# Two float32 transformer blocks in one program: the remaining projections in three rounded passes, split one job behind another, with a later bias table and two more expert buffers

## The chip, the cores and the metric

One core of a Trainium2 chip runs one program that computes both blocks. The metric is the device time of that program in microseconds (us). TensorE (PE) multiplies; VectorE (DVE), ScalarE (ACT) and GpSimd (POOL) do the elementwise work; SyncE (SP) issues nearly all DMAs.

## The reference, cut to what matters

All tensors are float32, with 256 tokens and a width of 1024. The first block has two layers of this form:

```python
for layer in range(2):
    u, q, k, v, g_pool, g_attn = split(rms(h, norm1) @ w_in)      # widths 1024, 3 x 1536, 1024, 1024
    pool_out = (centred_mean(u) - u) @ w_pool * pool_scale        # 4 groups of 256
    attn_out = dilated_attention(q, k, v, rel_bias)               # 12 heads of 128 in 3 groups, to 512
    h = h + (sigmoid(g_pool) * (pool_out @ w_a) + sigmoid(g_attn) * (attn_out @ w_b)) @ w_o
    a, gval = split(rms(h, norm2) @ w_up)                         # 2 x 2816
    h = h + (gelu(conv3(a)) * gval) @ w_down
```

The second block modulates its activations by `silu(c) @ w_ada`, mixes tokens in three ways, and ends in 32 experts of `(silu(x @ gate) * (x @ up)) @ down`, each 1024 by 512.

## The kernel before, in words

**Weights.** SP loads weights in blocks of 2 MB (`BLOCKS1`, L963) into `wring`, a ring of four slots (`SLOTS`). The load of block n waits until the last use of block n-4. `wb` blocks are half as large and `pool` blocks a quarter. Between the blocks of the first block lie twelve blocks `ada` of `w_ada`, which the second block needs; PE takes each in `modulate` (L1067) and adds it up in half of the PSUM tile `ps_s`.

**Jobs.** PE's work on a layer is a list of jobs (`layer_plan`). Each fills one of four PSUM banks, and begins when the bank of the job four places earlier is emptied. A layer has the jobs `x1` (transposes of the normed activations), 4 `u`, 6 `q`, 6 `k`, 6 `v`, 8 `gate` with the attention between them, 4 `pool`, 4 `wa`, 4 `wb`, 4 `wo`, `x2` (as `x1`), 22 `up` and 4 `down` that are accumulated in 11 rounds. Most jobs compute 256 output columns from half of a weight block, with K = 1024, which is eight tiles of 128 (`wb` has four).

**Split products.** The jobs u, q, k, v, up and down compute float32 products in three passes over rounded operands. ACT copies half a block, rounded, into `w_high` (two buffers, L1731, L1813); DVE subtracts it from the block to get `w_low` (L2106, L2202); activations are split into `x_high` and `x_low` in the same way. PE then makes three products for each tile (L1110): high by high, high by low, low by high. That is 48 matmuls of 256 columns for a job. ACT splits the weights of job n+2 as soon as job n is done. The jobs gate, pool, wa, wb and wo are ordinary float32 products (L1093, and L1199 for wo with 512 columns). The trace has two PE records for each float32 matmul, and one for each rounded matmul.

**Order at the norms.** After wo (or down), ACT squares the 256 by 1024 activations in two instructions and DVE scales them to `xs`. PE transposes them in the jobs x, ACT and DVE scale the transposed tiles out of PSUM into `xT`, ACT rounds all of it into `x_high` (L1738), and DVE subtracts it (L2111). Only then does the next product begin. PE takes three `ada` blocks ahead of these transposes, except in front of the first layer.

**Attention.** For each i of eight, PE computes `scores(i)`, the job `gate(i)`, the transposes of the probabilities of i-1 (`turn_probs`), and from the fourth on in every second the job `pv`. DVE does `logits(i)`: scale and bias (L2132), maximum, sign; after ACT's exponential it takes the reciprocal. ACT normalises (L1762), and takes the tanh of gate(i). DVE then copies the transposed probabilities of i-1 (`take_probT`, L2147). Each engine goes through its list strictly in order.

**Start.** Before layer 1 PE makes a table of attention biases; it goes out to DRAM, comes back with one row shifted per partition (`bias_table`), and PE mirrors it with twelve products by `flip`, which ACT copies out. DVE releases the first norm only then (L2042).

**Experts.** They are taken in eight turns of four, each turn with 12 blocks of 2 MB (L1017) in the four slots of `wring`. A load waits until `moe_used` says that its slot is free; the first four loads are released before the expert stage begins.

## Time and profile before

| | us |
|---|---|
| three runs | 2158.11, 2155.74, 2160.47 (median 2158.11) |
| the profiled execution's own time | 2155.31 |
| its span, first to last instruction | 2153.5 |
| PE busy | 1769.9 (82%) |
| DVE, ACT, POOL busy | 774.9 (36%), 545.7 (25%), 119.4 (6%) |

The mean granted TensorE clock is 0.925 of full speed. The program moves 417.76 MB by DMA, 194 GB/s on average. PE's busy share is an average over stages: in the first block PE is nearly always busy but at the norms and at the start, and in the expert stage it waits for weights. The part of the span outside of any stage below is the second block's mixing, which the change leaves in its order.

### The profile page before, as it was taken

The numbers are of one execution on the slowest core, as the hardware profiler recorded it, in microseconds if no ns is written. First come the engines' busy times: TensorE is split into PE (matmuls) and PEld (weight loads), VectorE is DVE, ScalarE is ACT, GpSimd is POOL, SyncE is SP. The second block draws the span as 40 slices with busy tenths as digits, with TensorE's granted clock in tenths as the row PEclk, the third lists the DMA queues.
The fourth block names the chain that finished last, engine by engine and source line by source line (L and its number), as shares of the span: only waits on it lengthen the run. The fifth ranks groups of instructions, "written<-read, shape, count | busy, mean of one in ns | idle before, by whom it ended". The sixth has DMA issues, their size and how long they took to land.

```text
span 2153.5 us, 30903 instructions
## 1 busy us (share of the span) xinstructions
PE 1769.9 (82%) x13683; PEld 1311.6 (61%) x13683; DVE 774.9 (36%) x1104; ACT 545.7 (25%) x708; POOL 119.4 (6%) x103
## 2 busy tenths in 40 slices
PE   2899997999799999799989998697984655566664
PEld 1899883997599987499767554486853111222221
DVE  0433212664434321366431744867533110111111
ACT  1443212543334320264321011333301100110110
POOL 0230000000041000000002410000000000000000
PEclk9899998999999999999999998798996888887898
DMA  6254156554755334575415110000033999999997
GB/s 238 102 177 163 50 176 258 200 179 155 274 192 176 121 108 181 197 260 211 178 57 142 64 39 10 1 3 2 32 137 128 409 409 409 410 409 391 405 409 298
DMA packets 154033, 417.76 MB, mean 194 GB/s; under 512 B 13799, under 2 KB 20746, under 8 KB 150847
## 3 DMA queue, kind: packets, MB, share of 16 engines
q1 hardware_dynamic: 151682, 412.65, 51.4%
q10 hardware_dynamic: 2236, 3.40, 0.5%
q8 instruction: 95, 1.56, 0.3%
q14 instruction: 20, 0.16, 0.0%
HBM read 414.14 MB, written 1.89 MB: 193 GB/s over the span
## 4 chain that ended last, share of the span: by engine, by line
PE 69%; DMA 21%; DVE 7%; ACT 2%; issue 2%; ACTq 0%; DVEq 0%; SPq 0%
PE bank L1110 24%; PE bank L1093 10%; DMA wring<-w_exp_down 7%; DMA wring<-w_exp_up 7%; PE bank L1229 6%; DMA wring<-w_exp_gate 4%; PE bank L1282 3%; PE bank L1199 3%; PE bank L1648 2%; PE bank L1307 2%; PE bank L1289 1%; PE ps_t L1282 1%; PE ps_t L1307 1%; PE ps_s L1307 1%; PE ps_s L1282 1%
## 5 line engine op out<-in xcount | busy, mean ns | idle before, releaser
L1110 PE MATMUL bank<-x_high,w_high 128*128 128x256 f32 x1216 | 346.3, 285 | 43.5 <-DVE x_low L2111 36.0
L1110 PE MATMUL bank<-x_low,w_high 128*128 128x256 f32 x1216 | 346.9, 285 | 0.0
L1110 PE MATMUL bank<-x_high,w_low 128*128 128x256 f32 x1216 | 340.2, 280 | 0.0
L2106 DVE TENSOR_TENSOR w_low<-wring,w_high 128x2048 fp32r<-128x2048 f32 x88 | 202.5, 2305 | 252.1 <-ACT w_high L1731 252.1
L1110 PEld LDWEIGHTS bank<-x_high,w_high 128*128 128x128 f32 x1216 | 231.2, 190 | 47.3 <-issue 47.3
L1110 PEld LDWEIGHTS bank<-x_high,w_low 128*128 128x128 f32 x1216 | 237.7, 195 | 0.0
L1731 ACT ACTIVATE w_high<-wring 128x2048 fp32r<-128x2048 f32 x88 | 168.6, 1920 | 271.9 <-PE bank L1110 263.2
L1110 PEld LDWEIGHTS bank<-x_low,w_high 128*128 128x128 f32 x1216 | 232.1, 191 | 0.0
L1648 PE MATMUL bank<-wring,R 128*32 128x512 f32 x1024 | 145.3, 707 | 89.5 <-DMA wring<-w_exp_up 76.0
L1093 PE MATMUL bank<-R,wring 128*128 128x256 f32 x704 | 155.2, 379 | 0.0
L1648 PEld LDWEIGHTS bank<-wring,R 128*32 128x32 f32 x1024 | 32.2, 122 | 196.3 <-DMA wring<-w_exp_up 116.1
L1093 PEld LDWEIGHTS bank<-R,wring 128*128 128x128 f32 x704 | 133.6, 190 | 18.1
L1664 PE MATMUL ps_s<-wring,R 128*32 128x512 f32 x256 | 48.2, 835 | 62.2 <-DMA wring<-w_exp_down 61.4
L2692 DVE TENSOR_TENSOR R<-bank,R 128x512 f32<-128x512 f32 x8 | 5.5, 692 | 227.1 <-PE bank L1648 227.1
L1282 PE MATMUL bank<-R,wring 128*128 128x512 f32 x176 | 79.4, 605 | 0.0
L1229 PE MATMUL bank<-w_high,a_high 128*128 128x512 f32 x176 | 70.1, 398 | 10.0 <-DVE R L2219 10.0
L2202 DVE TENSOR_TENSOR w_low<-wring,w_high 128x2048 fp32r<-128x2048 f32 x22 | 50.4, 2292 | 72.0 <-ACT w_high L1813 72.0
L2725 POOL TENSOR_TENSOR R<-R 128x542 f32<-128x542 f32 (+3 forms) x20 | 41.0, 2052 | 585.4 <-ACT R L1719 584.0
L1229 PE MATMUL bank<-w_low,a_high 128*128 128x512 f32 x176 | 70.0, 397 | 0.0
L1229 PE MATMUL bank<-w_high,a_low 128*128 128x512 f32 x176 | 69.8, 396 | 0.0
L1664 PEld LDWEIGHTS ps_s<-wring,R 128*32 128x32 f32 x256 | 5.7, 124 | 97.1 <-DMA wring<-w_exp_down 97.1
L1813 ACT ACTIVATE w_high<-wring 128x2048 fp32r<-128x2048 f32 x22 | 42.3, 1924 | 83.2 <-PE bank L1229 70.4
(549 smaller groups left out, 2683.0 us busy)
## 6 DMA issues: line engine op xcount, KB each, us to landing
wring<-w_in SPq DMA_DIRECT2D x37, 2048.0 KB, 8.1
wring<-w_exp_gate SPq DMA_DIRECT2D x32, 2048.0 KB, 17.4
wring<-w_exp_up SPq DMA_DIRECT2D x32, 2048.0 KB, 13.4
wring<-w_exp_down SPq DMA_DIRECT2D x32, 2048.0 KB, 17.5
wring<-w_up SPq DMA_DIRECT2D x22, 2048.0 KB, 9.0
wring<-w_ada SPq DMA_DIRECT2D x12, 2048.0 KB, 9.9
wring<-w_down SPq DMA_DIRECT2D x10, 2048.0 KB, 8.2
wring<-w_a SPq DMA_DIRECT2D x4, 2048.0 KB, 7.8
```

Of the source, the lines that this page charges most:

```text
L1093: mm = pe.matmul(b[:, i * S:(i + 1) * S], ww[:, wk0 + kk, c:c + P], rhs[0][:, rk0 + kk, :], start=kk == 0, stop=kk == rhs[1] - 1)
L1110: mm = pe.matmul(b[:, i * S:(i + 1) * S], left, right, start=k == 0 and m == 0, stop=k == KT - 1 and m == 2)
L1199: mm = pe.matmul(b[:, :], mT[:, k, t * P:(t + 1) * P], w(l, "wo", half, KT, 512)[:, k, :], start=k == 0, stop=k == KT - 1)
L1229: mm = pe.matmul(bank[JOB[("down", j)] % 4][:, :], left, ww[:, kk, half * 512:(half + 1) * 512], start=i == 0 and kk == 0 and m == 0, stop ...
L1282: mm = pe.matmul(b[:, i * width:(i + 1) * width], w2(n)[:, k, c:c + P], hT[:, k, 0:width], start=k == 0, stop=k == KT - 1)
L1307: mm = pe.matmul(b[q, 64 * o:64 * o + 64], lhs(q, c), rhs(q, c), start=start, stop=stop, skip_group_check=skip)
L1648: mm = pe.matmul(banks8[2 + which][q, :], xg[:, k, q], ww[:, u, k % 2, :], start=k == 0, stop=k == KT - 1)
L1664: mm = pe.matmul(banks8[5 + half][q, :], hidT[:, k, q], ww[:, u, half * 512:(half + 1) * 512], start=k == 0, stop=k == D_EXP // P - 1)
L1731: a.activation(w_high_r[:, n % 2, :, :], half_block(l, jobs[i], wring), ACT.Copy)\
L1813: a.activation(down_high(i), down_rows(l, i, wring), ACT.Copy).then_inc(w_high_ready, 1)
L2106: v.tensor_tensor(half_block(l, jobs[i], w_low), half_block(l, jobs[i], wring), w_high_r[:, n % 2, :, :].bitcast(F32), ALU.subtract).then_ ...
L2202: v.tensor_tensor(down_rows(l, i, w_low), down_rows(l, i, wring), down_high(i).bitcast(F32), ALU.subtract)\
```

## The change

1. The jobs gate, wa, wb and wo become split products too. One list `SPLITS` runs through u, q, k, v, gate, wa, wb, wo, up and down; ACT's `high(l, n)` and DVE's `low(l, n)` are called two jobs ahead everywhere. `split_rows` takes the operands, and alternates between the two halves of its bank in the innermost loop. pool stays float32.
2. The inputs of these products are split straight out of PSUM: ACT copies a bank, rounded, and DVE subtracts that from the same bank (`turned`, `pv_low`, and for the pooling output). The norms multiply by the gain before the transposes, in four products of 128x512 (`norm`, L2134 there), with the gain row loaded by DMA (`gain_row`). The squares are taken in pieces behind each job wo or down. A small Sqrt is put ahead of the place where the function table for it is needed.
3. The bias table is made behind the job u 3 of the first layer, with no mirroring; DVE reads it backwards. Its DMAs are issued by SP behind blocks k 0 and k 1.
4. `ada` blocks lie behind other blocks: two behind up 0 (or u 0) and one each behind the next two. PE takes two ahead of the transposes x2 (and x1 of the second layer) and two among the jobs.
5. `down` accumulates in `ps_s` and `ps_t`, and so does not wait for the banks of up.
6. The experts have six slots (`SLOTS_X`): two more in R, which grows by cutting the DMA scratch to 1024.

Cut to its core, the diff is:

```diff
+SLOTS, SLOTS_X = 4, 6
...
+DMA_SCRATCH = 1024
+R_SIZE = 36360
 
...
+    jobs = [("x1", j, "dve") for j in range(4)]
     jobs += [("u", j, "act") for j in range(4)]
...
 
 
 LAYER_BLOCKS = [("u", j, ("u", 2 * j + 1)) for j in range(2)]
@@ -94,14 +94,13 @@
 
     blocks = []
     for l in range(DEPTH):
+        behind = {}
+        if l:
+            behind.update({("u", 0): (4, 5), ("u", 1): (6,), ("q", 0): (7,)})
+        behind.update({("up", 0): (8 * l, 8 * l + 1), ("up", 1): (8 * l + 2,), ("up", 2): (8 * l + 3,)})
         for name, j, _ in LAYER_BLOCKS:
-            at = 2 * l + (name == "up") - 1
...
+SPLIT_MID = [(name, j) for name, n in (("gate", 8), ("wa", 4), ("wb", 4), ("wo", 4)) for j in range(n)]
 SPLIT_UP = [("up", j) for j in range(FT)]
 SPLIT_DOWN = [("down", i) for i in range(FT // 2)]
-SPLIT = {job: n for n, job in enumerate(SPLIT_IN + SPLIT_UP + SPLIT_DOWN)}
+SPLITS = SPLIT_IN + SPLIT_MID + SPLIT_UP + SPLIT_DOWN
+SPLIT = {job: n for n, job in enumerate(SPLITS)}
+NS = len(SPLITS)
...
+NORM_PARTS = (1, 4, 2, 4)
+SUMSQ_AT = [2 * sum(NORM_PARTS[:m]) for m in range(2 * DEPTH + 1)]
...
+        down_bank = [ps_s[:, 512:1024], ps_s[:, 0:512], ps_t[:, 0:512], ps_t[:, 512:1024]]
...
+            return (2 + m) % SLOTS_X
...
+            def gain_row(l, name):
+                sp.dma_start(grow, bass.AP(tensor=d[name].tensor, offset=l * D, ap=[[0, P], [1, D]])).then_inc(gain_in, 16)
...
+            gain_row(0, "norm1")
...
@@ -971,9 +1014,21 @@
                     for c, vec in enumerate(("c_2", "c_ctx_2")):
                         sp.dma_start(craw[:, c, :], bass.AP(tensor=d[vec].tensor, offset=0, ap=[[KT, P], [1, KT]]))\
                             .then_inc(craw_in, 16)
-                if (l, name, j) == (0, "up", 3):
+                if (l, name, j) == (0, "k", 0):
+                    sp.wait_ge(tab_ready, 1)
+                    sp.dma_start(tab_dram.rearrange("(g h) j -> h g j", h=4), tab[:, :, :]).then_inc(tab_out, 16)
+                if (l, name, j) == (0, "k", 1):
+                    sp.wait_ge(tab_out, 16)
+                    sp.dma_start(bias[:, :, :], bass.AP(tensor=tab_dram.tensor, offset=0,
+                                                        ap=[[1, P], [512, N_HEADS], [1, 384]])).then_inc(hankel_in, 16)
+                if (name, j) == ("wo", 1):
+                    wait_full(sp, l, ("pv", 3))
+                    gain_row(l, "norm2")
+                if (l, name, j) == (0, "up", 5):
+                    sp.wait_ge(xs_ready, 8)
+                    gain_row(1, "norm1")
                     set_out(0)
-                if (l, name, j) == (1, "q", 1):
+                if (l, name, j) == (1, "k", 1):
...
+                def split_rows(name, j, xh, xl, tokens_out=False, low_ready=None):
 
                     b = begin(name, j)
-                    ww = w(l, blk[0], blk[1], k, n)
-                    for i, c in enumerate((c0, c1)):
-                        for kk in range(rhs[1]):
...
-                    high, low = w_high_r[:, n % 2, :, :], half_block(l, (name, j), w_low)
-                    xh, xl = x_high_r, x_low_r
-                    for i in range(2):
-                        for k in range(KT):
-                            for m, (ww, xx) in enumerate(((high, xh), (high, xl), (low, xh))):
+                    wait_low(pe, l, (name, j))
+                    high, low = high_of(l, (name, j)), half_block(l, (name, j), w_low)
+                    last = k_tiles(name) - 1
+                    for k in range(last + 1):
+                        if low_ready and k % low_ready[1] == 0:
+                            pe.wait_ge(low_ready[0], l * HEADS_PER_GROUP + k // low_ready[1] + 1)
+                        for m, (ww, xx) in enumerate(((high, xh), (high, xl), (low, xh))):
+                            for i in range(2):
                                 part_of = slice(i * P, (i + 1) * P)
                                 left, right = (xx[:, k, part_of], ww[:, k, :]) if tokens_out else \
                                     (ww[:, k, part_of], xx[:, k, :])
-                                mm = pe.matmul(b[:, i * S:(i + 1) * S], left, right, start=k == 0 and m == 0,
-                                               stop=k == KT - 1 and m == 2)
+                                mm = pe.matmul(b[:, i * S:(i + 1) * S], left, right, start=k == 0 and m == 0 and i == 0,
+                                               stop=k == last and m == 2, skip_group_check=True)
+                    mm.then_inc(bank_full, 1)
...
-                pe.wait_ge(x_low_ready, l * 2 + 1)
...
+                for i in (8 * l, 8 * l + 1):
+                    modulate(l, i)
                 for j in range(4):
                     x_job("x2", j)
-                wait_emptied(pe, l, ("x2", 2))
-                wait_emptied(pe, l, ("x2", 3))
-                pe.wait_ge(x_low_ready, l * 2 + 2)
+                pe.wait_ge(x_low_ready, 4 * (2 * l + 2))
...
+            def high(l, n):
+
+                job = SPLITS[n]
+                wait_block(a, l, job[0], job[1] // 2)
+                if job[0] == "down":
+                    a.activation(down_high(l, job[1]), down_rows(l, job[1], wring), ACT.Copy).then_inc(w_high_ready, 1)
+                else:
+                    a.activation(high_of(l, job), half_block(l, job, wring), ACT.Copy).then_inc(w_high_ready, 1)
+
+            def root(l, n):
+                m = 2 * l + n
+                a.wait_ge(ms_ready, m + 1)
+                a.activation(stats[:, 12:14], stats[:, 10:12], ACT.Sqrt).then_inc(rms_ready, 1)
...
+            def turned(l, name, n):
+                for j in range(4):
+                    wait_full(a, l, (name, j))
+                    a.activation(half_tile(j, x_high), bank[JOB[(name, j)] % 4][:, :].rearrange("p (k s) -> p k s", s=P),
+                                 ACT.Copy).then_inc(x_high_ready, 1)
 
             for l in range(DEPTH):
...
+                a.activation(stats[:, 24:25], stats[:, 25:26], ACT.Sqrt)
+                for j in range(4):
+                    if j < 3:
+                        wait_full(a, l, ("wo", j))
+                        high(l, SPLIT[("wo", j)] + 2)
+                    wait_emptied(a, l, ("wo", j))
+                    for t in range(ST):
+                        c = slice(j * HALF, (j + 1) * HALF)
+                        a.activation(xn[:, t, c], h[:, t, c], ACT.Square, accum_out=stats[:, 4 * t + j:4 * t + j + 1]).then_inc(sumsq, 1)
+                root(l, 1)
+                turned(l, "x2", 1)
...
+            def low(l, n):
+
+                job = SPLITS[n]
+                wait_high(v, l, job)
+                if job[0] == "down":
+                    v.tensor_tensor(down_rows(l, job[1], w_low), down_rows(l, job[1], wring), down_high(l, job[1]).bitcast(F32),
+                                    ALU.subtract).then_inc(w_low_ready, 1)
+                else:
+                    v.tensor_tensor(half_block(l, job, w_low), half_block(l, job, wring), high_of(l, job).bitcast(F32),
+                                    ALU.subtract).then_inc(w_low_ready, 1)
...
+            def norm(l, n):
+
+                m = 2 * l + n
+                parts = NORM_PARTS[m]
+                v.wait_ge(sumsq, SUMSQ_AT[m + 1])
+                sums = stats[:, 0:2 * parts].rearrange("p (t c) -> p t c", t=ST)
+                if parts > 1:
+                    chain(v.tensor_reduce(stats[:, 8:10], sums, AX_X, ALU.add))
+                v.tensor_scalar(stats[:, 10:12], stats[:, 8:10] if parts > 1 else stats[:, 0:2], 1.0 / D, EPS, ALU.mult, ALU.add)\
+                    .then_inc(ms_ready, 1)
+                v.wait_ge(rms_ready, m + 1)
+                chain(v.reciprocal(stats[:, 14:16], stats[:, 12:14]))
+                v.wait_ge(gain_in, 16 * (m + 1))
+                for j in range(4):
+                    t, c = j // 2, slice((j % 2) * 512, (j % 2 + 1) * 512)
+                    v.scalar_tensor_tensor(xn[:, t, c], h[:, t, c], stats[:, 14 + t:15 + t], grow[:, c], ALU.mult, ALU.mult)\
+                        .then_inc(xs_ready, 1)
+
+            def turned(l, name, n):
+                for j in range(4):
+                    v.wait_ge(x_high_ready, 4 * (2 * l + n) + j + 1)
+                    v.tensor_tensor(half_tile(j, x_low), bank[JOB[(name, j)] % 4][:, :].rearrange("p (k s) -> p k s", s=P),
+                                    half_tile(j, x_high).bitcast(F32), ALU.subtract).then_inc(x_low_ready, 1)
+                v.wait_ge(x_low_ready, 4 * (2 * l + n) + 4)
+                for j in range(4):
+                    v.nop().then_inc(dve_emptied, 1)
 
             for l in range(DEPTH):
...
+                def pv_low(hh):
+                    v.wait_ge(at_high_ready, 4 * l + hh + 1)
+                    v.tensor_tensor(at_low[:, hh, :], bank[JOB[("pv", hh)] % 4][:, 0:S], at_high[:, hh, :].bitcast(F32),
+                                    ALU.subtract).then_inc(at_low_ready, 1)
+                    v.wait_ge(at_low_ready, 4 * l + hh + 1)
+                    v.nop().then_inc(dve_emptied, 1)
...
                     logits(i)
                     if i:
                         take_probT(i - 1)
+                    low(l, SPLIT[("gate", i)] + 2)
+                    if i % 2 == 0 and i >= 4:
+                        pv_low((i - 4) // 2)
...
+                def m_low(j):
+                    v.wait_ge(m_high_ready, 4 * l + j + 1)
+                    v.tensor_tensor(x_low[:, 2 * j:2 * j + 2, :], mT[:, 2 * j:2 * j + 2, :], x_high[:, 2 * j:2 * j + 2, :].bitcast(F32),
+                                    ALU.subtract).then_inc(m_low_ready, 1)
...
-                    wait_emptied(v, l, ("wa", j))
-                    v.tensor_tensor(m, m, tmp, ALU.add).then_inc(dve_emptied, 1)
                     wait_emptied(v, l, ("wb", j))
+                    v.tensor_tensor(m, m, tmp, ALU.add).then_inc(m_ready, 1)
+                    v.wait_ge(m_ready, 4 * l + j + 1)
+                    low(l, SPLIT[("wb", j)] + 2)
+                    if j:
+                        m_low(j - 1)
+                m_low(3)
                 for j in range(4):
...
+            v.memset(st[:, 61:62], 0.0).then_inc(moe_used, 2)
...
+    nc = bacc.Bacc("TRN2", target_bir_lowering=False, num_devices=1, dynamic_dma_scratch_size=DMA_SCRATCH)
```

DVE in the attention. Here is one i of the eight before: logits (four rows) and `take_probT`.

```order
L2132 SCALAR_TENSOR_TENSOR R<-ps_s,R 128x768
L2137 TENSOR_REDUCE stats<-R 128x1
L2138 TENSOR_SCALAR stats<-stats 128x1
L2140 RECIPROCAL stats<-stats 128x1
L2147 COPY R<-ps_t 128x6x128
```

And here is one i in the changed kernel, with the first row of the next.

```order
L2169 SCALAR_TENSOR_TENSOR R<-ps_s,R 128x768
L2174 TENSOR_REDUCE stats<-R 128x1
L2175 TENSOR_SCALAR stats<-stats 128x1
L2177 RECIPROCAL stats<-stats 128x1
L2184 COPY R<-ps_t 128x6x128
L2116 TENSOR_TENSOR w_low<-wring,w_high 128x8x256
L2169 SCALAR_TENSOR_TENSOR R<-ps_s,R 128x768
```

The subtraction for gate(i+2) now stands between the logits of i and those of i+1.

DVE at the second norm of a layer before, from the last updates of h by wo to the first jobs up.

```order
L2174 SCALAR_TENSOR_TENSOR h<-bank,h 128x512 x4
L2082 TENSOR_SCALAR stats<-stats 128x2
L2084 RECIPROCAL stats<-stats 128x2
L2086 TENSOR_SCALAR xs<-h,stats 128x1024 x2
L2106 TENSOR_TENSOR w_low<-wring,w_high 128x8x256 x2
L2095 TENSOR_SCALAR R<-bank,R 128x256 x4
L2111 TENSOR_TENSOR x_low<-R,x_high 128x2048
```

The same place in the changed kernel.

```order
L2243 SCALAR_TENSOR_TENSOR h<-bank,h 128x2x256
L2126 TENSOR_REDUCE stats<-stats 128x2
L2127 TENSOR_SCALAR stats<-stats 128x2
L2130 RECIPROCAL stats<-stats 128x2
L2134 SCALAR_TENSOR_TENSOR R<-h,stats,R 128x512 x4
L2140 TENSOR_TENSOR x_low<-bank,x_high 128x4x128 x4
L2116 TENSOR_TENSOR w_low<-wring,w_high 128x8x256 x2
```

The two weight subtractions no longer stand ahead of the activations' own, and scaling out of PSUM is gone.

SP's loads around the beginning of up in the first layer, before (b_ada is a small bias, `modulation` the result of four `ada` blocks going out).

```order
L963 DMA wring<-w_o 128x8x512 x2
L884 DMA R<-b_ada 128x1x512
L963 DMA wring<-w_ada 128x2x2048 x3
L963 DMA wring<-w_up 128x8x512
L963 DMA wring<-w_ada 128x2x2048
L963 DMA wring<-w_up 128x8x512 x3
L889 DMA modulation<-R 128x512
L963 DMA wring<-w_up 128x8x512 x7
```

And in the changed kernel.

```order
L1002 DMA wring<-w_up 128x8x512
L918 DMA R<-b_ada 128x1x512
L1002 DMA wring<-w_ada 128x2x2048 x2
L1002 DMA wring<-w_up 128x8x512
L1002 DMA wring<-w_ada 128x2x2048
L1002 DMA wring<-w_up 128x8x512
L1002 DMA wring<-w_ada 128x2x2048
L1002 DMA wring<-w_up 128x8x512 x3
L984 DMA R<-norm 128x1024
L923 DMA modulation<-R 128x512
L1002 DMA wring<-w_up 128x8x512 x5
```

The block up 2 now stands behind an `ada` block that waits for the slot of up 0, and the outgoing `modulation` stands behind up 5.

## Rows read from the trace of the kernel before

**Rows 1.** The page: shares of the chain that ended last, by engine and line.

```profile
PE 69%; DMA 21%; DVE 7%; ACT 2%; issue 2%; ACTq 0%; DVEq 0%; SPq 0%
PE bank L1110 24%; PE bank L1093 10%; DMA wring<-w_exp_down 7%; DMA wring<-w_exp_up 7%; PE bank L1229 6%; DMA wring<-w_exp_gate 4%; PE bank L1282 3%; PE bank L1199 3%; PE bank L1648 2%; PE bank L1307 2%; PE bank L1289 1%; PE ps_t L1282 1%; PE ps_t L1307 1%; PE ps_s L1307 1%; PE ps_s L1282 1%
```

**Rows 2.** Busy time by stage: stretch, length, engines, granted PE clock, DMA share, GB/s.

```profile
0.00:67.00 67.00, 19.42 (x48) 9.63 (x48) 12.62 (x18) 18.23 (x27) 2.10 (x5) 0.90 0.55 191
67.00:194.00 127.00, 126.50 (x1056) 126.29 (x1056) 46.43 (x20) 49.11 (x42) 32.61 (x18) 0.99 0.47 166
194.00:273.00 79.00, 78.81 (x389) 69.64 (x390) 24.52 (x39) 23.05 (x37) 0.00 (x0) 1.00 0.23 77
283.00:324.00 41.00, 41.00 (x191) 35.78 (x189) 6.89 (x10) 1.53 (x3) 0.00 (x0) 1.00 0.44 152
324.00:354.00 30.00, 28.42 (x73) 12.37 (x76) 4.08 (x6) 0.00 (x0) 0.00 (x0) 1.00 0.43 170
354.00:374.00 20.00, 6.76 (x61) 3.09 (x54) 10.18 (x12) 10.86 (x13) 0.00 (x0) 0.76 1.00 377
374.00:503.00 129.00, 128.58 (x1072) 126.65 (x1072) 79.37 (x85) 62.47 (x65) 0.00 (x0) 0.98 0.53 189
503.00:508.00 5.00, 0.40 (x1) 0.40 (x2) 3.34 (x3) 2.46 (x3) 0.00 (x0) 0.96 0.82 301
570.00:591.00 21.00, 7.73 (x66) 3.62 (x67) 10.78 (x13) 11.01 (x14) 0.00 (x0) 0.80 1.02 387
591.00:720.00 129.00, 129.00 (x1072) 127.27 (x1070) 47.03 (x21) 48.65 (x41) 32.68 (x18) 0.98 0.53 188
1658.00:2138.00 480.00, 296.02 (x1850) 92.18 (x1854) 48.59 (x114) 45.50 (x73) 0.00 (x0) 0.85 1.01 402
```

**Rows 3.** The start: waits until 67 us (total, times, longest), and the first weight block's landing.

```profile
PE bank L1053 <- DMA R<-bias_table: 21.9, 1, 21.9
wring<-w_in SPq DMA_DIRECT2D x1, 2048.0 KB, 13.0
```

**Rows 4.** PE's pace: L1110 in 100 us of up, and L1093 in the attention.

```profile
400.00:500.00 100.00, 100.00 (x849) 99.84 (x849) 1.00 0.60 214
L1093 PE MATMUL bank<-R,wring 128*128 128x256 f32 x257 | 56.9, 379 | 0.0
```

**Rows 5.** Groups of the page and of the attention: count, busy, mean ns, idle before.

```profile
L2106 DVE TENSOR_TENSOR w_low<-wring,w_high 128x2048 fp32r<-128x2048 f32 x88 | 202.5, 2305 | 252.1 <-ACT w_high L1731 252.1
L1731 ACT ACTIVATE w_high<-wring 128x2048 fp32r<-128x2048 f32 x88 | 168.6, 1920 | 271.9 <-PE bank L1110 263.2 <-DMA wring<-w_up 5.9 <-DMA wring<-w_in 2.8
L2132 DVE SCALAR_TENSOR_TENSOR R<-ps_s,R 128x768 f32<-128x768 f32 x8 | 7.7, 957 | 21.3 <-PE ps_s L1120 21.3
L1758 ACT ACTIVATE R<-R,stats 128x768 f32<-128x768 f32 x8 | 7.5, 935 | 25.6 <-DVE stats L2138 25.6
L2140 DVE RECIPROCAL stats<-stats 128x1 f32<-128x1 f32 x8 | 1.3, 164 | 8.8 <-ACT R L1758 8.8
```

**Rows 6.** The timeline: start, length, engine, instruction. A gate's tanh, a modulation block, an update of h, squares.

```profile
228.61 0.60 ACT L1719 ACTIVATE R<-bank 128x512 f32<-128x512 f32 x1 [2.48 <-PE bank L1093]
...
387.16 1.92 PE L1067 MATMUL ps_s<-wring,R 128*32 128x512 f32 x16
...
353.38 0.69 DVE L2174 SCALAR_TENSOR_TENSOR h<-bank,h 128x512 f32<-128x512 f32 x1 [6.17 <-PE bank L1199]
...
354.11 1.06 ACT L1701 ACTIVATE R<-h 128x1024 f32<-128x1024 f32 x1 [69.55 <-DVE h L2174]
```

**Rows 7.** The ring's transfers issued at 350 to 380 us: time to landing.

```profile
DMA to landing us min/median/max: 7.7/12.7/18.2
```

**Rows 8.** SP's timeline: issues of the experts' loads.

```profile
1557.12 59.12 SPq L1017 DMA_DIRECT2D wring<-w_exp_gate  x4
1660.35 5.53 SPq L1017 DMA_DIRECT2D wring<-w_exp_up  x4
```

590 lines of the change are left out of this document (268 added, 322 removed).

## The prediction

> **What bounds the kernel now.** I began with the chain that ended last. It runs over PE for 69% and over DMA for 21% of the span, and of the DMA part the experts' weights make 18% [rows 1]. So there are two regimes. The busy times by stage show them [rows 2]. In the first block PE is busy in 126.5 of 127 us of the stage u to v, in 78.8 of 79 us of attention and in 128.6 of 129 us of up: there only fewer or shorter matmuls help. Between those stages lie holes: 67 us before the first projection, 20 us from the end of wo to up, 21 us in front of the second layer, 5 us from up to down. In the experts, from 1658 to 2138 us, DMA runs at 402 GB/s while PE is busy for 296 of 480 us: there only bytes that are already loaded help. The second block's mixing, which lies between, keeps its order, and I count nothing for it.
>
> PE's pace comes from two rows [rows 4]: 849 matmuls in 100 us are 117.8 ns each for a rounded pass, and 56.9/257 = 221 ns for each of the two records of a float32 product. A job of K = 1024 is therefore 32 x 0.221 = 7.07 us in float32 and 48 x 0.1178 = 5.65 us in three passes.
>
> **The change, part by part.** I write each stage of the first block as it is and as it should become; the boundaries of before are those of the stretches in [rows 2], with the tenths (within 0.6 us of them) from the first and last matmul of each stage.
>
> *Start.* The long wait ahead of the first projection is for the bias table's way through DRAM, 21.9 us [rows 3], with twelve mirroring products and then the norm behind it. All of the table goes behind u 3. What is late next is the first weight block: it landed 13.0 us after its issue at 1.25 us [rows 3], behind 1 MB of h and some small constants. In the new order h and a gain row of 0.5 MB stand in front of it, so I take 13.5 us. Behind it lie ACT's rounding (1.9, [rows 5]), four copies out of PSUM (0.6 each, as the tanh in [rows 6]) and four subtractions of 128x512 (0.69 each, as the update of h in [rows 6]), which DVE starts when it is through with the weights: 13.5 + 1.9 + 2.4 + 2.8 = 20.6. The norm itself is hidden under the landing. 67.0 becomes 20.6: **-46.4**.
>
> *u to v.* The table now costs PE three float32 products of 512 columns, 6 records of 0.44, and two small transposes: **+3** in the first layer. The way through DRAM has some 90 us until attention needs it and is hidden.
>
> *Attention, both layers.* Eight gates save 8 x 1.42 = 11.4 us of PE. But ACT and DVE get 1.9 and 2.3 us of splitting for each [rows 5], and both work in strict order. One i then closes into a ring: tanh 0.60, rounding 1.92, subtraction 2.30, bias 0.96, maximum 0.95, sign 0.15, exponential with its sum 1.12, reciprocal 0.16, normalising 0.94, and ACT is back at the next tanh. (The maximum and the normalising are instructions of 768 elements like those beside them.) These sum to 9.1; with six handovers of 0.04 it is 9.3 us. PE needs 5.65 + 1.33 + 0.66 = 7.6 us for an i without pv and 10.3 with it, so ring and PE bound it nearly equally. The stage also starts later: gate 1 is rounded and subtracted in front of the evacuation of v 5 and in front of logits 0, and PE waits for that evacuation, 3.9 us from the end of v against 0.7. From there 7.0 us to the end of gate 0, seven turns of 9.3 and the last transposes give 76.1; it was 79.4. **-3.3 each**, not -11.4. pool grows by 0.3 each, since its banks are now emptied by DVE: **+0.3 each**.
>
> *wa and wb.* Before, 41 us at full speed [rows 2] (41.5 to the end of wb); now 4 x 5.65 + 4 x 2.83 = 33.9, and 0.2 of waits: **-7.4 each**. ACT and DVE owe 1.9 and 3.0 us for a job of 5.65, so wa hides them.
>
> *wo.* In wb DVE owes 2 x 0.69 of its own per job, then subtractions of 1.2, 1.2, 2.3 and 2.3 us, then 0.69 for each part of the new input: 14.6 us against PE's 11.3. It is late, and wo 0 waits for it: 1.5 us before it starts and 2.3 in its middle. 4 x 5.65 + 3.8 = 26.4 against 29.3: **-2.9 each**.
>
> *Norms.* From wo to up: update of h 0.69, squares of the last piece 1.15 (two of a quarter of the length in [rows 6], each with its sum), four small steps with handovers 1.0, then four products of 0.69 and, as soon as ACT has the last copies under way, four subtractions of 0.69: 8.5 us. Transposes and modulation (two blocks of 1.9, [rows 6]) lie underneath. It was 20.5: **-12.0** in each layer, and **-11.4** in front of layer 2.
>
> *ada blocks and the ring.* One block more per group stands among the jobs: **+1.9** three times. And the order of loads bites. The block up 2 (q 0) waits behind an ada block, which waits for the slot of up 0 (u 0), so until up 1 (u 1) is done. From there a first transfer needs 7.7 us and the longest of a queue of four 18.2 although some began later [rows 7]; I take 7.7 and 5.4 for each further. up 2 lands at 13.1, rounding and subtraction end at 17.4, and PE, which had two jobs and one modulation to do, is there at 13.3: **+4** in three places. In the first layer SP also waits behind up 5 until the modulation's sum is taken in job 8; the next blocks land late by **+2.3**. PE should see less of the cold start, **-1** in each of three places: the hole before up in which its clock fell to 0.76 of full speed [rows 2] is over 10 us long, and would be 2.
>
> *up to down.* Other banks: the 5 us [rows 2] go, **-5.3 each**.
>
> *Experts.* Two more blocks lie ready when PE begins. The first load that PE's use releases stays at 1660.35 [rows 8], so two blocks fewer of 2.10 MB at 409 GB/s follow: 2 x 5.13 = 10.3 us. The stream also has holes: 480 us at 402 instead of 409 GB/s are up to 8, of which I give six slots half, 3.7: **-14.0**.
>
> *Nothing:* cutting the DMA scratch, reading the bias backwards, the moved Sqrt. No row prices the first two; DVE has room for a slower read of the bias only up to 0.2 us per i, since it stands in the ring above.
>
> Sum. Layer 1: -46.4 + 3 - 3.3 + 0.3 - 7.4 - 2.9 - 12.0 + (1.9 + 4 + 2.3 - 1) - 5.3 = -66.8. Layer 2: -11.4 + (1.9 + 4 - 1) - 3.3 + 0.3 - 7.4 - 2.9 - 12.0 + (1.9 + 4 - 1) - 5.3 = -32.2. Experts: -14.0. Together -113, from the profiled execution's own 2155.3: **2042**. That execution lies 2.8 below the median of the three runs shown, so I say 2043.
>
> By the Trainium skill ("FP8 and Floating Point Precision", TensorE Precision Notes) true FP32 takes four passes through the array, so three passes would be three quarters of it: a job of 5.30 us. The rows above have 5.65, because a rounded pass runs at 117.8 ns and a pass of float32 at 110.5. With the page's ratio the 36 jobs' worth of K = 1024 that change would give another 12 us; the trace disagrees, and I follow the trace.
>
> **The bounds of what no row shows.** Alternating between two halves of a bank: from nothing up to no overlap of weight loads with matmuls; I take nothing, since up runs with PEld busy 99.84 of 100 us [rows 4] and still at the full pace, but this is the only price that could undo everything. Subtracting out of PSUM with an input from SBUF: 0.69 as for h. Multiplying by a gain row: also 0.69. The six slots: between 0 and 18 us. The ring of attention: between PE's pace (-11.4 per layer) and one more microsecond per i (+8).
>
> **The rivals.**
> - *The three passes pay in full* (0.12). ACT and DVE keep ahead in attention, where they were idle for most of the 79 us [rows 2]; -8 more per layer, 2027. Against it: strict order makes their idle time useless to each other.
> - *The experts gain nothing* (0.10). The DMA share is 1.01 throughout [rows 2], so the stream could be bound from an earlier point. Against it: the four loads ahead are issued at 1557 to 1616 and the stream only begins at 1660 [rows 8], so the queue is idle before. 2057.
> - *The ring of weights starves PE more than I see* (0.14): an ada block in front of a projection costs 10 us rather than 4 in three places, or DVE's debt in wb carries on through wo. 2062.
> - *The new order of matmuls breaks their overlap* (0.03), slower. 5952 rounded matmuls of the first block would run in the new order. The saving is gone at 113/5952 = 19 ns each, a pace of 137 ns; at 190, the length of a weight load, it would be 430 us slower.
> - *My sum as it stands* (0.58), by itself 2030 to 2056. The remaining 0.03 is for anything else.
>
> **How the numbers follow.** The predicted time is that of my sum. The range takes in the first three rivals in large part: 2020 to 2066. A measurement of this kernel tells about 0.2%, 4.3 us, from no change. Only the fourth rival and part of the rest end above: faster 0.96, same 0.01, slower 0.03.
>
> **What would show it.** Each step has its place in the changed profile: the first split matmul at about 21 us, and 130 us from there to the end of v; scores of the attention 9.3 us apart on average, with DVE and ACT taking turns, and 76 us in all; wo 0 waiting for DVE's subtraction; 8.5 us from wo to up with ends of x_low on the chain; a wait of 4 us for w_low ahead of up 4 and q 0, and in the first layer near up 12; no wait between up and down; six expert blocks ahead of about 1550 us and a stream at 409 GB/s. The prediction is wrong by tens of microseconds if the pace of L1110's successor is not 118 ns, if attention takes 85 us or more, or if the second block's mixing changes its length.

## The result, and the profile after

The changed kernel takes 2051.2 us, median of 4 runs (2048.63 to 2052.29), beside 2159.29 us for the kernel before on the same chip: a ratio of 0.9499, 95% interval 0.9482 to 0.9517. The prediction was 2043 us with a range of 2020 to 2066. The profiled execution took 2050.65 us, 104.7 less than that of before; its span is 2048.9.

The page's chain that ended last, shares by engine and by line:

```profile
PE 62%; DMA 19%; DVE 11%; ACT 5%; issue 3%; DVEq 0%; SPq 0%; ACTq 0%
PE bank L1159 28%; DMA wring<-w_exp_down 9%; DMA wring<-w_exp_up 6%; PE ps_s L1267 3%; PE ps_t L1267 3%; PE bank L1345 3%; PE ps_s L1320 2%; PE bank L1320 2%; ACT w_high L1725 2%; PE bank L1670 2%; DVE w_low L2116 2%; PE bank L1686 2%; DMA wring<-w_up 2%; DMA wring<-w_in 2%; PE ps_t L1327 1%
```

Against [rows 1] DVE went from 7 to 11% and ACT from 2 to 5%: the splits now stand on the path in places. The busy time by stage, columns as in [rows 2]: start, u to v, attention, wa and wb, wo, norm, up, down, then two pieces of up behind its wait, one from its undisturbed part, and the experts' stream:

```profile
0.00:21.00 21.00, 3.89 (x17) 3.55 (x18) 8.13 (x14) 10.61 (x13) 2.11 (x5) 0.93 0.93 328
21.00:152.00 131.00, 131.00 (x1064) 128.50 (x1064) 53.12 (x25) 50.62 (x43) 30.29 (x18) 0.97 0.60 210
152.00:228.00 76.00, 70.78 (x515) 67.57 (x515) 42.40 (x49) 36.58 (x45) 0.00 (x0) 0.98 0.27 94
238.00:272.00 34.00, 33.99 (x288) 33.81 (x287) 17.89 (x19) 13.68 (x13) 0.00 (x0) 1.00 0.54 196
272.00:299.00 27.00, 23.70 (x198) 22.95 (x201) 16.34 (x14) 12.17 (x19) 0.00 (x0) 1.00 0.59 200
299.00:307.00 8.00, 6.14 (x52) 2.97 (x45) 6.04 (x12) 5.11 (x10) 0.00 (x0) 1.00 0.76 262
307.00:443.00 136.00, 129.90 (x1085) 126.38 (x1085) 81.32 (x86) 62.07 (x65) 0.00 (x0) 0.99 0.61 223
443.00:505.00 62.00, 61.88 (x268) 49.52 (x266) 28.34 (x17) 23.95 (x16) 0.00 (x0) 1.00 0.52 182
337.00:339.00 2.00, 2.00 (x12) 2.00 (x11) 2.00 (x2) 0.66 (x2) 0.00 (x0) 0.53 1.05 386
339.00:341.00 2.00, 2.00 (x19) 2.00 (x19) 1.93 (x5) 0.00 (x0) 0.00 (x0) 1.00 1.05 387
400.00:440.00 40.00, 40.00 (x342) 40.00 (x341) 24.67 (x22) 17.47 (x16) 0.00 (x0) 1.00 0.57 207
1577.00:2033.00 456.00, 280.53 (x1754) 96.75 (x1750) 48.59 (x113) 44.31 (x71) 0.00 (x0) 0.85 1.02 408
```

The 67 us at the start are 21, the 20 us of the norm are 8, and wa and wb have no hole. But up is busy in 129.9 of 136 us where it was in 128.6 of 129, and attention in 70.8 of 76 where it was in 78.8 of 79. PE's waits from 21 to 1005 us (engine, tile and line, then whom it waited for: total, times, longest):

```profile
PE bank L1159 <- DVE w_low L2116: 17.0, 5, 5.6
PE bank L1159 <- DVEq L2144: 6.1, 1, 6.1
PE bank L1159 <- DVE x_low L2140: 5.5, 3, 1.8
PE ps_t L1190 <- ACT R L1753: 5.1, 2, 2.6
PE ps_s L1181 <- ACT R L1742: 5.0, 2, 2.5
PE bank L1159 <- DVE x_low L2218: 3.4, 2, 1.7
PE bank L1159 <- issue: 3.2, 2, 1.6
PE ps_s L1181 <- DVE R L2169: 0.3, 2, 0.2
```

The first row is the weights ring: five waits for a low part, 4.2, 5.3 and 5.6 us at up 4, q 0 and up 4 and two near up 12. The second is the end of the start. Rows four and five are the last and the first step of attention, six and seven lie in and before wo 0.

Stage by stage, in us, from the first and last matmul of each (stages with the same code vary by up to 1.6 between executions, with PE's clock behind a wait):

| stage | before | predicted | after |
|---|---|---|---|
| start | 67.0 | -46.4 | -46.2 |
| u to v, first layer | 126.5 | +3 | +4.8 |
| attention, layer 1 | 79.4 | -3.3 | -3.3 |
| attention, layer 2 | 79.5 | -3.3 | -2.7 |
| wa and wb, each layer | 41.4 | -7.4 | -7.2 |
| wo, each layer | 29.3 | -2.9 | -2.9 |
| wo to up, each layer | 20.5 | -12.0 | -12.7 |
| down 1 to u, layer 2 | 20.6 | -11.4 | -12.6 |
| up, layer 1 | 128.7 | +7.2 | +8.1 |
| u to v, layer 2 | 129.5 | +4.9 | +6.5 |
| up, layer 2 | 128.3 | +4.9 | +9.3 |
| up to down, each | 67.3 | -5.3 | -5.3 |
| first block in all | 1095.9 | -99 | -91.3 |
| experts, from their first product | 495.1 | -14.0 | -13.1 |

### The profile page after: what moved, and what is told of

Read it like the earlier page. It is cut to its first block, busy times and chain, and to the rows that moved or that the text cites. A ratio compares the mean times of both kernels' runs of the same rounds, so it can differ in the third digit from the quotient of the medians.

```text
span 2048.9 us, 32409 instructions
## 1 busy us (share of the span) xinstructions
PE 1719.2 (84%) x14363; PEld 1328.0 (65%) x14363; DVE 870.9 (43%) x1183; ACT 607.3 (30%) x771; POOL 114.9 (6%) x103
## 4 chain that ended last, share of the span: by engine, by line
PE 62%; DMA 19%; DVE 11%; ACT 5%; issue 3%; DVEq 0%; SPq 0%; ACTq 0%
PE bank L1159 28%; DMA wring<-w_exp_down 9%; DMA wring<-w_exp_up 6%; PE ps_s L1267 3%; PE ps_t L1267 3%; PE bank L1345 3%; PE ps_s L1320 2%; PE bank L1320 2%; ACT w_high L1725 2%; PE bank L1670 2%; DVE w_low L2116 2%; PE bank L1686 2%; DMA wring<-w_up 2%; DMA wring<-w_in 2%; PE ps_t L1327 1%
## 5 line engine op out<-in xcount | busy, mean ns | idle before, releaser
L2116 DVE TENSOR_TENSOR w_low<-wring,w_high 128x2048 fp32r<-128x2048 f32 (+1 forms) x128 | 287.2, 2244 | 338.8 <-ACT w_high L1725 338.2
L1725 ACT ACTIVATE w_high<-wring 128x2048 fp32r<-128x2048 f32 (+1 forms) x128 | 238.1, 1860 | 362.6 <-PE bank L1159 317.9
L1686 PEld LDWEIGHTS bank<-wring,R 128*32 128x32 f32 x768 | 23.9, 119 | 159.9 <-DMA wring<-w_exp_up 106.2
L2113 DVE TENSOR_TENSOR w_low<-wring,w_high 128x2048 fp32r<-128x2048 f32 x22 | 50.4, 2293 | 60.1 <-ACT w_high L1723 60.1
L1159 PE MATMUL bank<-w_high,x_high 128*128 128x256 f32 x320 | 64.3, 282 | 6.6 <-DVE x_low L2218 3.4
L1670 PE MATMUL bank<-R,xs 128*128 128x128 f32 x256 | 43.8, 349 | 26.3 <-DVE R L2744 26.3
L1159 PE MATMUL bank<-w_high,x_low 128*128 128x256 f32 x320 | 64.2, 282 | 0.0
L1159 PE MATMUL bank<-w_low,x_high 128*128 128x256 f32 x320 | 63.9, 281 | 0.0
L1723 ACT ACTIVATE w_high<-wring 128x2048 fp32r<-128x2048 f32 x22 | 42.2, 1916 | 70.9 <-PE ps_t L1267 58.0
L1320 PE MATMUL bank<-R,wring 128*128 128x256 f32 (+1 forms) x192 | 52.9, 433 | 2.2 <-ACT R L1889 1.1
L1159 PEld LDWEIGHTS bank<-w_high,x_high 128*128 128x128 f32 x320 | 49.5, 190 | 7.4 <-DVE x_low L2218 3.8
```

The costliest lines, as they stand in the source:

```text
L1159: mm = pe.matmul(b[:, i * S:(i + 1) * S], left, right, start=k == 0 and m == 0 and i == 0, stop=k == last and m == 2, skip_group_check=True)
L1320: mm = pe.matmul(b[:, i * width:(i + 1) * width], w2(n)[:, k, c:c + P], hT[:, k, 0:width], start=k == 0, stop=k == KT - 1)
L1670: mm = pe.matmul(banks8[j][:, i * P:(i + 1) * P], xs[:, t, k * P:(k + 1) * P], pick[:, t, :], start=t == 0, stop=t == ST - 1)
L1686: mm = pe.matmul(banks8[2 + which][q, :], xg[:, k, q], ww[:, u, k % 2, :], start=k == 0, stop=k == KT - 1)
L1723: a.activation(down_high(l, job[1]), down_rows(l, job[1], wring), ACT.Copy).then_inc(w_high_ready, 1)
L1725: a.activation(high_of(l, job), half_block(l, job, wring), ACT.Copy).then_inc(w_high_ready, 1)
```

## The experiments

Each was built from the changed kernel. For small effects the median of four runs says little (executions of one kernel differ by 3 to 13 us), so I give the median and then the stage in the trace, where the effect stands alone. "Less" and "more" compare medians with the changed kernel's 2051.2. The kernel before had a median of 2159.3 us beside the changed kernel, and of 2158.0, 2157.7, 2154.5 and 2157.6 beside the four groups of experiments, so medians of different groups compare to about 5 us: by the ratios e_order is 7.6 us less rather than 10.9, and e_ring_before 15.5 more rather than 13.0. The intervals of e_ring_late, e_ring_late2, e_ring_before, e_slots4, e_order and best lie clear of the changed kernel's; those of the other six overlap it.

**The ring of weights, one place later** (e_ring_late).

```
-  {("u", 0): (4, 5), ("u", 1): (6,), ("q", 0): (7,)}       # ada blocks behind a block
-  {("up", 0): (8l, 8l+1), ("up", 1): (8l+2,), ("up", 2): (8l+3,)}
+  {("u", 0): (4, 5), ("q", 0): (6,), ("q", 1): (7,)}
+  {("up", 0): (8l, 8l+1), ("up", 2): (8l+2,), ("up", 3): (8l+3,)}
   # modulate behind q 1 and q 3, up 5 and up 7; the sums taken one job later
```

> One part changed: in the weights ring the third and fourth ada block of each set are loaded one place later (behind the third and fourth block of up, behind the first two blocks of q), and PE multiplies them after up 5 and up 7, after q 1 and q 3. Theory 1 (the three waits of PE in front of up 4, q 0 and up 4, 4.2, 5.3 and 5.6 us in the trace of the changed kernel, are the ring's: a block of up or q is loaded only when an ada block ahead of it has gone, and comes 5.1 us later for each): each shrinks to about 1 us, and the slow clock behind each (the first two jobs of the next 13.1 to 13.2 us where two take 11.4) goes with it: 3 x 4 + 3 x 1.7 = 17 us, so 12 to 19 us less. Rival (the waits are VectorE's or ScalarE's own debt from the norm in front of up and u, and would be there whatever the ring does): 0 to 3 us less, the waits in the same places. Second rival (the later ada multiplies lie in front of other blocks and move the wait to q 4 and up 8): no change, with waits of 4 to 5 us at q 4 and up 8.

2040.8 us (2037.9 to 2044.3), ratio 0.9456 (0.944 to 0.9472), 10.4 less. The waits at up 4, q 0 and up 4 fell from 4.2, 5.3 and 5.6 to 1.39, 1.41 and 1.37 us: the first theory, though the gain is less than the 12 to 19 us that it gave. For a wait of 7.6 us came ahead of up 12 in the first layer, which none of the three theories had. What SP waits for between 300 and 400 us in this kernel shows it:

```profile
SPq L1002 <- PE bank L1159: 43.6, 5, 20.5
SPq L923 <- DVE R L2106: 26.8, 1, 26.8
SPq L1002 <- PE ps_s L1123: 1.5, 1, 1.5
```

L923 stores the first modulation sum. For 26.8 us nothing behind it is issued, though slots are free; four loads of up then go out one behind another. In the changed kernel the same row reads 22.9 us.

**The same, and the store moved** (e_ring_late2).

```
-                if (l, name, j) == (0, "up", 5):
+                if (l, name, j) == (0, "up", 8):
                     set_out(0)
```

> As the run with the ada blocks one place later, and besides SP stores the first modulation sum behind the load of the ninth block of up (up 8), not of the sixth (up 5). Theory 1 (in that run SP waited from 348 to 375 us for the sum, with the loads of four blocks of up queued behind it, and PE waited 7.6 us for the seventh block in front of up 12; the same wait is the 1.1 and 0.8 us of the changed kernel at up 12 and 13): the 7.6 us go and nothing comes in their place, so 7 to 9 us less than that run, 17 to 20 us less than the changed kernel. Rival (the blocks are late there by VectorE's work in the first half of up, which makes the parts too late whatever the loads do): the wait at up 12 stays at 3 us or more.

2030.0 us (2027.6 to 2032.6), ratio 0.940 (0.9374 to 0.9426): 21.2 less than the changed kernel. SP waits 4.6 us for the sum, PE waits nowhere near up 12, and its waits for a low part are now three:

```profile
PE bank L1160 <- DVE w_low L2117: 4.5, 3, 1.7
```

up and u to v of the second layer shrank by 15.6 us in the trace. The waits are 12.5 of them; the other 3 are the clock behind a long wait. In the changed kernel PE had been idle for 4.2 us ahead of 335.4, and the granted clock then was 0.53 from 337 to 339 us, that is nearly all at the lower level of 1.2 GHz, and 1.00 from 339 on (two rows of the stages above, with 12 and 19 matmuls in 2 us). Matmuls start 0.213 us apart until then and 0.119 behind it, and the first two jobs take 13.0 us; they take 13.1 and 13.0 behind the waits of 5.3 and 5.6 us. Behind this kernel's wait of 1.39 us the same place reads:

```profile
331.80:333.80 2.00, 2.00 (x18) 2.00 (x19) 1.93 (x5) 1.89 (x4) 0.00 (x0) 1.00 1.05 387
```

and the two jobs take 11.5. So in these places a wait of 4 us costs 1.5 us more than its length, one of 1.4 us nothing more. Length alone does not decide in between. Behind the norm PE waits 1.84 us for the last low part each time; in the changed kernel the next two jobs then take 11.4 us at 306.5 and at 513.4, and 12.9 at 805.3, where the granted clock fell to the lower level:

```profile
807.00:809.00 2.00, 2.00 (x11) 2.00 (x11) 1.19 (x1) 0.00 (x0) 0.00 (x0) 0.50 0.04 9
```

And behind the 2.5 us ahead of the first scores of attention, the second scores start 8.7 us after the first in the changed kernel and 7.1 us in e_start, with the same code.

**The ring as before** (e_ring_before): three ada blocks ahead of up 0 and of the second layer's u 0, one behind, multiplied where they were.

```
-  {("up", 0): (8l, 8l+1), ("up", 1): (8l+2,), ("up", 2): (8l+3,)}    # behind
+  {("up", 0): (8l, 8l+1, 8l+2)}                                     # ahead
+  {("up", 0): (8l+3,)}                                             # behind; u 0 likewise
```

> One part undone: three ada blocks stand ahead of the first block of up and of the second layer's u, and one behind it, as in the kernel before, with the ada multiplies where they stood before. Theory 1 (the new order of the ring is needed because a half-block is now split two jobs ahead: high(up 0) stands in ScalarE's order behind wo 2, and its block would now land only after wo 3, with the squares of the norm queued behind it): no waits at up 4 and q 0 (15.1 us and about 5 us of slow clock less), but 10 to 12 us more between the last wo and up 0 in both layers and at the second layer's x1: 10 to 20 us more in all. Rival (the new order brings only the waits at up 4 and q 0, and the old one would be as good for the splits): 15 to 20 us less.

2064.2 us (2062.5 to 2065.6), ratio 0.9571 (0.9555 to 0.9587): 13.0 more. The waits in front of up and u (from the same view of waits, this kernel):

```profile
PE bank L1142 <- DVE R L2134: 20.9, 2, 10.6
PE ps_s L1123 <- DVE h L2301: 12.9, 1, 12.9
...
PE bank L1159 <- DVE w_low L2116: 2.1, 2, 1.3
```

The stages up and u to v get 27 us shorter (the low parts are waited for 2.1 us, not 17.0), the three norms 42 us longer, from 7.8 and 8.0 to 21 and 24. So the new order of the ring is the price of splitting two jobs ahead, and a cheap one; it is not a blemish beside it.

**Four slots** (e_slots4).

```
-SLOTS, SLOTS_X = 4, 6
+SLOTS, SLOTS_X = 4, 4          # and R's two slots are not announced as free
```

> One part undone: the experts' weights turn through four slots, not six. Theory 1 (the two added slots let two more 2 MB blocks in ahead of the router and fill the holes of the stream): 13 to 14 us more, the last landing of an expert block that much later, holes of the stream back in the places where they were before. Rival (the experts' stretch came out shorter since the stream met less other traffic or began earlier, and the slots are worth nothing): 0 to 2 us more.

2068.7 us (2062.6 to 2075.4), ratio 0.9585 (0.9556 to 0.9614): 17.5 more. The experts' stream in this kernel, to be read beside the last row of stages above:

```profile
1579.00:2055.00 476.00, 293.33 (x1770) 94.16 (x1774) 48.54 (x113) 44.36 (x71) 0.00 (x0) 0.83 0.99 396
```

It moves at 396 GB/s, not 408, and lasts 476 us, not 456. Two blocks more in the stream are 10.2 us; steps between landings of 6.3 to 11.7 us instead of 5.1, in five places, make another 14.6 in this execution. Before, holes of that kind made 3.7. The four executions spread over 13 us, those of the changed kernel over 4; but with six slots e_start and e_table_first spread over 9 us, so it is not shown that the spread comes from the holes.

**Order on the small engines in attention** (e_order).

```
# ScalarE, behind each job of u to v
-                    high(l, i + 2)
+                    if (name, j) != ("v", 5): high(l, i + 2)
                     evac(name, j, ...)
+                    if (name, j) == ("v", 5): high(l, i + 2)
# VectorE, attention
                     logits(i)
                     if i: take_probT(i - 1)
+                    if i == 7: low(l, SPLIT[("gate", 6)] + 2)
-                    low(l, SPLIT[("gate", i)] + 2)
+                    if i != 6: low(l, SPLIT[("gate", i)] + 2)
```

> Two places of the order on the small engines: ScalarE takes v 5 out of its bank before it splits the half-block behind it, and VectorE makes the low part for wa 0 behind the seventh probabilities and not ahead of the last logits. Theory 1 (attention is bound by PE for every i but the last, and only these two places wait: 2.5 us between v 5 and the first scores, 2.6 us in front of the last turned probabilities, in each layer): 1.9 + 2.5 us less in each layer, 8.8 in all, 6 to 10. Rival (attention is bound by a ring of ScalarE and VectorE of 9.3 us for each i, as my prediction had it, so that what is saved at its last place is lost at the next one, in pool or wa 0): 4 us less at most, all of it at v 5.

2040.3 us (2039.9 to 2044.0), ratio 0.9464 (0.9448 to 0.9479): 10.9 less. Attention went from 76.3 and 76.9 us to 71.2 in each layer and nothing came back in pool or wa, as the first theory said. The stage got shorter at its two ends: the first scores start 0.75 us behind v and not 2.5, and the ring's last turn, without the 2.3 us of wa 0's half-block, is 4.8 us long and not 9.6. All that PE waits for in the 71.2 us of layer 1 is this:

```profile
PE ps_s L1181 <- DVE R L2172: 0.9, 2, 0.4
PE ps_s L1181 <- ACT R L1742: 0.7, 1, 0.7
```

So 69.6 us are PE's own work here. The theory's reason, that PE bounds all turns but the last, is half of the matter, as the next experiment shows: with PE's work taken away the ring still holds the stage.

**The gates in two passes** (e_two_pass). Left out is the third pass of the eight gate jobs.

```
-  for m, (ww, xx) in enumerate(((high, xh), (high, xl), (low, xh))):
+  passes = ((high, xh), (high, xl), (low, xh))[0:2 if name == "gate" else 3]
+  for m, (ww, xx) in enumerate(passes):
```

> The eight gate jobs leave out their third pass (the low part of the weights against the high part of the input), which is part of the computation; all rounding, subtracting and waiting stays. PE has 8 x 1.9 = 15.2 us less work in the attention of each layer. Theory 1 (attention is held by one ring through ScalarE and VectorE of 8.9 us without and 9.6 us with pv, nine tenths of PE's 8.9 on average): with PE's own work for an i at 5.7 and 8.3 us the starts of the logits stay 8.9 to 9.6 us apart or go down only where the ring held a wait for the gate; the stage goes from 76.3 (74.7 in other executions) to 72 to 75 us, so 2 to 8 us less in all, and PE waits in every turn. Rival (PE bounds attention but for its last turn, so the third pass is paid in full, as the case of three passes paying in full had it): 12 to 15 us less in each layer, 24 to 30 us in all, with logits 6 to 7.5 us apart.

2047.6 us (2044.7 to 2048.5), ratio 0.9495 (0.9478 to 0.9511), too little for runs. Of 15.2 us less work in each layer the stages kept 2.9 and 2.5 us. The logits of this kernel in layer 1, and who waited for them; then PE's waits for them in both layers (total, times, longest):

```profile
L2170 DVE SCALAR_TENSOR_TENSOR R<-ps_s,R x8: 948/950/958, 155.3 to 219.2; 128x768 f32<-128x768 f32 x8
...
who waited for it (us, times):
  PEld ps_s L1182: 11.0, 5
  PE ps_s L1182: 9.6, 5
```

```profile
PE ps_s L1182 <- DVE R L2170: 18.7, 9, 3.0
```

and of the changed kernel:

```profile
L2169 DVE SCALAR_TENSOR_TENSOR R<-ps_s,R x8: 950/951/958, 157.6 to 223.1; 128x768 f32<-128x768 f32 x8
```

The eight starts span 63.9 us with two passes and 65.4 with three. The difference is the first step, 8.95 and 10.47; the others are the same to 0.01, 8.94 without pv's subtraction and 9.58 with it. Five sixths of the third pass were free. So the ring through ACT and DVE sets the pace as soon as PE is quicker, as predicted. With three passes the two are close: PE's own work is 71.1 of the 76.3 us, it may run one i ahead, and it waits 0.3 us for logits in all, so the ring is not seen before the last turn.

**Where wo 0 waits** (e_debt, e_wo_order). In e_debt the addition of the second projection to m is left out.

```
-  v.tensor_tensor(m, m, tmp, ALU.add).then_inc(m_ready, 1)
+  v.memset(stats[:, 26 + j:27 + j], 0.0).then_inc(m_ready, 1)
```

> In wb VectorE leaves out the addition of the second projection to the first (m keeps the first product alone; a memset of one column takes its place and signals), which is part of the computation. Theory 1 (the two waits of PE in wo 0, 1.6 and 1.7 us in each layer, are VectorE's debt from wb, where it has 14.6 us of work against PE's 11.3): with 4 x 0.63 us less of it both waits shrink, to 0 to 1 us together, so 2.3 to 3.3 us less in each layer, 5 to 7 in all. Rival (the waits come from a longer ring with ScalarE: rounding of wo's half-blocks and of m, each behind a wait): they stay, and the change is below 2 us.

2050.8 us (2046.1 to 2051.9), ratio 0.9494 (0.9467 to 0.9522). The first wait stayed at 1.61 us, the second went from 1.71 to 1.12 and 1.43: 0.9 us of the 5 to 7 expected. The theory of a debt fell. The timeline of the changed kernel shows what is there (PE's other rows left out):

```profile
269.41 1.92 ACT L1725 ACTIVATE w_high<-wring 128x2048 fp32r<-128x2048 f32 x1 [1.00 <-PE bank L1159]
...
271.43 2.29 DVE L2116 TENSOR_TENSOR w_low<-wring,w_high 128x2048 fp32r<-128x2048 f32 x1 [0.50 <-ACT w_high L1725]
...
273.82 0.48 PE L1159 MATMUL bank<-w_high,x_high 128*128 128x256 f32 x2 [1.59 <-issue]
...
275.68 2.29 DVE L2116 TENSOR_TENSOR w_low<-wring,w_high 128x2048 fp32r<-128x2048 f32 x1
...
277.89 1.28 DVE L2218 TENSOR_TENSOR x_low<-R,x_high 128x512 fp32r<-128x512 f32 x2
278.62 0.50 PE L1159 MATMUL bank<-w_high,x_high 128*128 128x256 f32 x2 [1.71 <-DVE x_low L2218]
```

wb 2 ends at 269.4; only then may its buffer take the half-block for wo 0, and 1.92 + 2.29 us later PE begins. Between lies one job of wb, 2.8 us long: 1.6 us of latency, whatever DVE owes. DVE's reported idle of 0.50 in front of that subtraction says the same. The second wait is order: m's third quarter stands behind the 2.29 us for wo 1. So e_wo_order:

```
# ScalarE, for j of wb; then behind the loop
-                    high(l, SPLIT[("wb", j)] + 2)
+                    if j < 3: high(l, SPLIT[("wb", j)] + 2)
+                high(l, SPLIT[("wb", 3)] + 2)
# VectorE, for j of wb; then behind m_low(3)
-                    low(l, SPLIT[("wb", j)] + 2)
+                    if j < 3: low(l, SPLIT[("wb", j)] + 2)
+                low(l, SPLIT[("wb", 3)] + 2)
```

> Behind the last job of wb, ScalarE rounds m's last quarter ahead of the half-block for wo 1, and VectorE makes the low parts of m 2 and m 3 ahead of that half-block's. Theory 1 (formed after the run without the addition: the wait ahead of wo 0 is the rounding and subtraction of its half-block, 1.9 + 2.3 us from the end of wb 2 against one job of 2.8; the wait within wo 0 is the low part of m 2, which stands behind the 2.3 us for wo 1): the 1.6 us ahead of wo 0 stay, the 1.7 us within it go, 3.4 us less in all, 2 to 4. Rival (VectorE's debt from wb, whatever its order): the wait within wo 0 stays above 1 us or comes back at wo 1; 0 to 1 us less.

2048.9 us (2045.1 to 2050.4), ratio 0.9504 (0.9487 to 0.9521), too little for runs. In the trace the 1.60 ahead of wo 0 stays, the 1.7 within it are gone and 0.89 came in front of wo 1: 0.7 to 0.8 us less in each layer. The first theory named the cause and missed what is late next.

**Order of the matmuls** (e_outer).

```
-  for k ...: for m, (ww, xx) ...: for i in range(2):
+  for i in range(2): for k ...: for m, (ww, xx) ...:
```

> One part undone: the 48 matmuls of a split job write one half of the bank and then the other, as before, not both in turn (weight tile by weight tile the work is the same). Theory 1 (the order has no price: the pace of 119 ns a matmul is the slow half of the clock and the array itself): the jobs stay at 5.7 us; only where a job begins with inputs not yet there (wa 0, wb 0, wo 0 wait for the low part piece by piece) all pieces are wanted in half the time, so up to 1.4 us more in wo 0 and 0.5 in wa 0 of each layer, 0 to 4 us more in all. Rival (taking turns between two halves is what keeps the pace): the jobs grow by 5 ns a matmul or more, 30 us and up. Second rival (taking turns costs): 5 us less or more than that.

2056.1 us (2052.2 to 2059.5), ratio 0.953 (0.9504 to 0.9555): 4.9 more, which the runs alone do not tell from nothing. No pace changed; u to v of the first layer took 130.1 us, as in three other kernels with the order unchanged. The wait within wo 0 went from 1.7 to 3.2 us in both layers, since one half of the bank wants all of m in half the time; that is 3 of the 4.9 us, and the rest is not told from the spread. (The expectation calls 119 ns a matmul the slow half of the clock. The rows have a granted clock of 1.00 at this pace, as from 400 to 440 us, and 0.213 us a matmul at the lower level.)

**The table first** (e_table_first): loads and products of the bias table ahead of the first block and of u 0.

```
+            (the loads of rel_bias, c_hot, c_inv and the small vectors)
             for n, (l, name, j) in enumerate(BLOCKS1):
...
+                if l == 0:
+                    bias_table()
                 pe.wait_ge(x_low_ready, 4 * (2 * l + 1))
```

> One part undone: the products of the bias table, the transposes of the small vectors and the loads of both stand in front of the first weight block and of u 0, not behind u 3; the way of the table through DRAM stays where it is in the changed kernel. Theory 1 (the 46 us of the start were the table's way through DRAM and what was queued behind it, not its products or its loads): 14 more issues of 0.4 us in front of the first block, and the products in the gap that it leaves, so the first split matmul 5 to 9 us later and u to v 3 us shorter: 2 to 7 us more. Rival (the loads and products themselves held the start, with the small vectors' many descriptors): 15 to 45 us more.

2053.6 us (2049.8 to 2059.3), ratio 0.9518 (0.9487 to 0.955). The first split matmul is at 24.7, not 20.75, and u to v takes 127.1 us instead of 131.3 (130.1 in other executions), so where products and loads stand is worth 1 us at most. That leaves 42 of the 46 us to what this run did not bring back: the way through DRAM, the mirroring and what was queued behind them.

**Inputs first** (e_start).

```
-  if l == 0: high(l, 0)          # DVE: low(l, 0)
   turned(l, "x1", 0)
+  if l == 0: high(l, 0)
```

> At the start ScalarE and VectorE split the turned inputs first and the half-block for u 0 behind them. Theory 1 (the last thing before the first split matmul is the input's low part, made at 18.1 to 20.6 us behind the half-block's, while the turned inputs lie ready from 12 to 14.7 us): copies to 15.2, the half-block rounded to 17.1 and subtracted to 19.4, the first split matmul about 1.2 us earlier. Rival (the first block's landing at 13.9 sets the start, and the half-block's splitting behind it is the shortest way): as much later as the copies last, 1 to 2 us more.

2050.3 us (2046.8 to 2056.0), ratio 0.952 (0.9499 to 0.9541). The first split matmul is at 19.27 us, 1.5 earlier. The runs can't tell that; the trace can.

**All together** (best): the edits of e_ring_late2, e_order, e_wo_order and e_start in one kernel.

> All that the experiments point to together: the ada blocks one place later and the first modulation sum stored behind up 8 (21 us less than the changed kernel), the two places of order in attention (11 less), the order behind wb (3.4 less), the inputs first at the start (1.2 less). If the places are independent: 36 us less, 2015 us. If the gains overlap (the ring of weights then waits for PE in other places, since PE comes earlier): 25 us less or fewer, 2026 us, with new waits of PE in up or q to v.

2022.1 us, median of 5 (2020.5 to 2025.3), ratio 0.9381 (0.9368 to 0.9393): below both kernels, and 29.1 below the changed one (25.5 if both are scaled by their kernels of before). The first block keeps everything: 973.3 us against 1004.6, 31.3 less, where the stages changed one by one had given 15.6, 10.9, 1.5 and 1.5 us, 29.5 in all. The profiled execution then gives 2.0 us back in the mixing and 4 at its end. Its stream, and the 12 us behind the last landing:

```profile
1550.00:2003.00 453.00, 329.24 (x1734) 115.97 (x1734) 48.53 (x113) 44.31 (x71) 0.00 (x0) 0.69 1.02 409
2003.00:2015.00 12.00, 9.60 (x24) 2.93 (x24) 3.44 (x5) 0.60 (x1) 0.00 (x0) 0.59 0.00 0
```

The granted clock was 0.69 over the stream and 0.59 behind it. The stream is DMA's, 409 GB/s, and did not notice; the last products took 9.6 us of PE where they took 5.6 in the changed kernel, and the end came 4 us later. Two of the five runs had a mean clock of 0.895 and 0.909 and took 2025.3 and 2023.7 us; the three at 0.933 took 2020.5 to 2022.1.

## Why the prediction was right, point by point

*The sum.* The parts add up to -113.0 us for the profiled execution, and 104.7 were measured, so 8.3 were missing. The three stages with the weights ring gave 6.9 us less than predicted, u to v of the first layer 1.8, and the other stages some 2 together; the three norms gave 2.6 more, which is luck. The prediction also goes from 2042 to 2043 for an offset of 2.8 us, which makes 2045.

*The two regimes.* Right. Fewer passes paid in wa, wb and wo, bytes loaded ahead in the experts, and the mixing between kept its length: the offset between the two traces is 91.3 us at its start and 91.6 at the first product of the experts.

*Start.* Right in size and cause: the block landed at 13.94 (13.5 predicted), the splitting ended at 20.6. One term was another than I wrote: behind ACT's rounding stood DVE's subtraction of the half-block, 2.3 us, and not the four copies, 2.4, which ran beside it. e_table_first shows that the place of loads and products hardly mattered. I took as given that the weights are split before the inputs; e_start shows 1.5 us in that.

*u to v, first layer.* +4.8 against +3. The table cost 3.1; the rest is the clock, granted at 0.97 over the stage where it was 0.99 [rows 2]. With the same code the stage took 130.1 us in other executions, which is +3.6.

*Attention.* Right in mechanism. The ring is there in the order that I gave, and e_two_pass shows that it holds the stage when PE has less to do. That 9.34 us lie between logits on average, as in my sum, is partly luck: a turn takes 8.94 us, 9.58 with the subtraction of pv, which I had left out, and the first one 10.47. My terms also add to 76.8 us with the 0.8 of the last transposes, not to 76.1. Two parts were off against each other: the scores start 2.5 us after v 5 rather than 3.9, and PE waits 2.6 us in front of the last transposes, which I had inside the ring. The rival that the three passes pay in full is refuted for this kernel: they brought 3.3 and 2.7 us of 11.4, and a whole pass less 2.7 of 15.2. But I called ring and PE nearly equal and then priced the ring alone. With two places of the order changed (e_order) the stage is 8.2 us shorter than before, so most of the loss lay in those two places. Reading the bias backwards cost nothing, as assumed: the instruction takes 0.951 us where it took 0.957. No run tells the price of the smaller DMA scratch.

*wa and wb, norms, up to down.* Right within 1.2 us each. The norms came out at 7.8 us and not 8.5: the squares took 0.9 us and not 1.15, the small steps 0.8 and not 1.0, the four subtractions 2.5 and not 2.8.

*wo.* The size was right, 26.4 us, with waits of 3.3 us and not 3.8. The step behind it was half wrong: "14.6 us against PE's 11.3. It is late, and wo 0 waits for it". The first wait is the latency of one split against a half-length job, the second is order (e_debt, e_wo_order).

*The weights ring.* This is the term that was mis-sized. I had, in each of three places, 4 us of wait and 1 us back from the clock at the start of the stage. The waits were 4.2, 5.3 and 5.6 us, 3 more in all; and each wait made a cold start of its own, 1.5 to 1.6 us that I had not counted: together +23.9 us in these three stages against +17.0. The clock at the start of the stages gave back 1.9, 2.7 and 0 us, more in all than the 3 that I took. I knew the clock's price from the old hole and did not put it on my own wait. The mechanism was right: e_ring_late and e_ring_late2 took it out. So was the piece on SP behind up 5, 2.3 predicted and 1.9 measured. The rival of a ring that starves PE by 10 us in each place did not come: with its slow start a wait cost 5.8 to 7.2 us, between my 4 and its 10. Nor did its other half, the debt of wb.

*Experts.* 13.1 us against 14.0, from 10.2 for two blocks and the rest from holes, which made 3.7 us before and none after; e_slots4 confirms the cause and gives it 17.5 us, more than before had to lose, as holes came larger there. The rival that experts gain nothing is refuted.

*The order of matmuls.* e_outer shows no change of pace either way. By the Trainium skill ("FP8 and Floating Point Precision", TensorE Precision Notes), with four passes for true FP32, a job of three passes had come to an estimated 5.30 us, three quarters of 7.07. In the changed kernel 40 us of up hold 342 matmuls, those that touch its ends counted: 117 ns each or 5.6 us a job. The trace agrees with [rows 4] and not with that ratio.

## What to carry to other kernels

When splitting or conversion moves to helper engines that work in strict order, add up their loop for one turn, hand-overs included, and compare it with the matmul engine's: if the two are near each other the busy share of the matmul engine looks full and yet matmuls are free; leaving a third of them out is the test. Then look at the two ends of the loop: here the order in two places was worth 5 us a layer. When a load is wanted one job earlier than before, walk through the ring's order of loads again, with each store that stands in the same queue: a store that waits for a result (L923) holds every load behind it, and curing a wait in the ring only showed that one. Last, a wait can cost more than its length, so price one of several microseconds with the slow jobs behind it.

## What the runs showed that I had not expected

- After TensorE had been idle for 4.2 to 5.6 us its matmuls started at the lower clock level, 0.213 us apart, for some 3.5 us, and only then 0.119 us apart; after the waits of 1.4 us all started at 0.12. Waits of 1.84 and 2.5 us went either way with the same code (11.4 or 12.9 us for two jobs, 7.1 or 8.7 us between scores).
- The clock over the same experts' stream was 0.85 in the changed kernel and 0.69 in one execution of the last one, at 408 and 409 GB/s: while the stream is DMA's the lower clock costs nothing here, and only the 12 us behind it lengthen, by 4 us. Why it was lower there is not settled.
- With four slots the stream has holes of up to 6.6 us over the usual step in the trace, with six there are none.
